# Decay steps and an expert's turning placed later, a copy placed earlier, and idle turnings on TensorE, in a streaming-encoder step

## The reference

```python
h = rms_norm(x, norm_mix); z = h @ w_in
qa, ka, va, ra, da, qb, kb, vb, ga, gb = split(z)
log_a = log_sigmoid(da @ w_decay + b_decay) / 16        # decay of the gated linear attention
o_a, s_new = gla_scan(qa, ka, va, log_a, s0)            # uses cumsum(log_a) in exponentials
...                                                     # second attention branch, gates, two projections
x = x + mix @ w_out
g = argmax over 4 groups; two best of the 4 experts in it; weights from two softmaxes
y[t] = sum over the token's 2 experts e of w * ((silu(x_t @ w_gate[e]) * (x_t @ w_up[e])) @ w_down[e])
x = rms_norm(x + y, norm_final)
```

## Time and profile before

| | before |
|---|---|
| runs (3) | median 1045.04 us, 1044.43 to 1046.35 |
| profiled execution | 1044.21 us, its span 1042.5 us |
| mean granted TensorE clock | 0.993 |
| PE busy | 1009.4 us (97%) |
| PE weight loads (PEld) | 897.5 us (86%) |
| DVE / ACT / POOL busy | 661.4 (63%) / 540.9 (52%) / 166.3 (16%) us |
| moved over the span | 207.55 MB, mean 199 GB/s |

### The profile page before, as it was taken

The page is one execution under the profiler, slowest core; times in us unless marked ns, Lnnn a source line. Parts: engine busy times, 40 slices in busy tenths (PEclk is TensorE's granted clock), DMA queues, the critical chain, the costliest instruction groups (busy, mean ns, idle before and its releaser), DMA issues.

```text
span 1042.5 us, 16960 instructions
## 1 busy us (share of the span) xinstructions
PE 1009.4 (97%) x6950; PEld 897.5 (86%) x6950; DVE 661.4 (63%) x995; ACT 540.9 (52%) x720; POOL 166.3 (16%) x178
## 2 busy tenths in 40 slices
PE   6999899999999999999999999999999999999995
PEld 5999899998999988888989899878778888888884
DVE  5334753453223356767665656356898898889896
ACT  5236533432223244545474553233677878887874
POOL 2111100000000123432331020013211011010162
PEclk9999999999999999999999999999999999999998
DMA  8877865527355465475464271616999999999976
GB/s 190 199 219 175 163 144 67 95 46 117 54 69 102 111 120 70 76 61 70 114 194 148 65 254 35 242 81 234 413 412 413 413 414 414 413 414 413 415 158 155
DMA packets 126171, 207.55 MB, mean 199 GB/s; under 512 B 11229, under 2 KB 68573, under 8 KB 126098
## 3 DMA queue, kind: packets, MB, share of 16 engines
q1 hardware_dynamic: 110290, 149.38, 53.3%
q0 software_dynamic: 13168, 47.59, 13.4%
q10 hardware_dynamic: 2640, 9.57, 2.3%
HBM read 174.40 MB, written 32.12 MB: 198 GB/s over the span
## 4 chain that ended last, share of the span: by engine, by line
PE 85%; DVE 6%; ACT 4%; issue 3%; DMA 2%; ACTq 0%; POOL 0%; DVEq 0%; POOLq 0%
PE ps L1248 23%; PE ps L1250 23%; PE ps L1249 23%; PE ps L1222 5%; PE ps L1406 2%; PE ps L1420 2%; DMA x_rows<-h,slot_i 2%; PE ps L1382 1%; ACT w_hi L848 1%; PE ps L1366 1%; PE ps L1521 1%; PE ps L1381 1%; PE ps L1318 1%; DMA xg<-x_rows 1%; DVE x L2273 0%
## 5 line engine op out<-in xcount | busy, mean ns | idle before, releaser
L1960 DVE TENSOR_TENSOR e_lo<-raw,e_hi 128x2048 fp32r<-128x2048 f32 x96 | 219.3, 2288 | 28.1 <-ACT e_hi L1031 27.9
L1031 ACT ACTIVATE e_hi<-raw 128x2048 fp32r<-128x2048 f32 x96 | 184.1, 1918 | 55.0 <-PE ps L1250 44.4
L1248 PE MATMUL ps<-h_hi,w_hi 128*128 128x272 f32 x632 | 186.7, 295 | 0.0
L1250 PE MATMUL ps<-h_hi,w_lo 128*128 128x272 f32 x632 | 182.3, 288 | 0.0
L1249 PE MATMUL ps<-h_lo,w_hi 128*128 128x272 f32 x632 | 181.9, 288 | 0.0
L1746 DVE TENSOR_TENSOR w_lo<-ring,w_hi 128x2048 fp32r<-128x2048 f32 (+1 forms) x40 | 72.5, 1812 | 79.9 <-ACT w_hi L848 79.9
L848 ACT ACTIVATE w_hi<-ring 128x1024 fp32r<-128x1024 f32 (+1 forms) x56 | 79.6, 1422 | 82.3 <-PE ps L1250 67.3
L1248 PEld LDWEIGHTS ps<-h_hi,w_hi 128*128 128x128 f32 x632 | 119.1, 188 | 1.2 <-issue 0.7
L1249 PEld LDWEIGHTS ps<-h_lo,w_hi 128*128 128x128 f32 x632 | 119.1, 189 | 0.2
L1250 PEld LDWEIGHTS ps<-h_hi,w_lo 128*128 128x128 f32 x632 | 118.8, 188 | 0.0
L1248 PE MATMUL ps<-w_hi,h_hi 128*128 128x256 f32 x384 | 109.4, 285 | 2.6 <-DVE va L2031 2.6
(11 more groups left out here) (418 smaller groups left out, 2038.8 us busy)
## 6 DMA issues: line engine op xcount, KB each, us to landing
raw<-in_w_gate_dram SPq DMA_DIRECT2D x32, 1024.0 KB, 10.3
raw<-in_w_up_dram SPq DMA_DIRECT2D x32, 1024.0 KB, 8.8
raw<-in_w_down_dram SPq DMA_DIRECT2D x32, 1024.0 KB, 9.3
ring<-in_w_in_dram SPq DMA_DIRECT2D x24, 1024.0 KB, 10.8
x_rows<-zero POOLq DMA_DIRECT2D x16, 512.0 KB, 8.0
ring<-in_w_in_dram SPq DMA_DIRECT2D x16, 512.0 KB, 8.4
xg<-x_rows POOLq DMA_DIRECT2D x15, 512.0 KB, 6.3
y_rows<-yo ACTq DMA_DIRECT2D x14, 512.0 KB, 6.6
```

Of the source, the lines that this page charges most:

```text
L1031: act.activation(e_hi[buf][:], raw[slot][:], ACT.Copy).then_inc(s_ehi, 1)
L1248: pe.matmul(out, left[0], right[0], start=first, stop=False)
L1250: return pe.matmul(out, left[1], right[0], start=False, stop=final)
L1960: dve.tensor_tensor(e_lo[slot][:], raw[slot][:], e_hi[buf][:].bitcast(F32), ALU.subtract).then_inc(s_elo, 1)
```

## The change

Four things. Two decay hooks, 3 and 4, hang behind units two later than before. ACT copies `g_row` before its second block of squares. On PE, `idle_turns` adds transposes of the identity whose results nobody uses: 44 in the entry and 10 in the last routing step. For that the wait for the identity comes first, and those ahead of the fourth tile, which write the gain's bank, wait until `g_row` is copied. In the second expert's preparation, product 3 of expert 0 comes ahead of the turning of expert 1's rows, on ACT and DVE one split of weights does so too, `rows_index` moves behind `gated`, and `overflow_counts` into expert 1.

```diff
--- before.py
+++ after.py
@@ -395,7 +395,7 @@
         hook(units_of["ra"][-1], "gate_s")
         for f in range(GH + 2):
             if f <= GH:
-                hook(units_of["va"][2 * f], "dec", f)
+                hook(units_of["va"][(0, 2, 4, 8, 10)[f]], "dec", f)
             if f >= 2:
                 hook(units_of["va"][2 * f + 1], "dec_apply", f - 2)
         for i in range(NTILE):
@@ -871,9 +871,9 @@
                 act.activation(h_hi[:, :, t0:t0 + n], ps[:, b:b + 2].rearrange("p b (c t) -> p (b c) t", t=P)[:, :, 0:n], ACT.Copy).then_inc(s_xhigh, 1)
 
             x_squares(0)
-            x_squares(1)
             act.wait_ge(s_gmix, 17)
             act.activation(g_row[:], ps[:, 0:2].rearrange("p b n -> p (b n)"), ACT.Copy).then_inc(s_gmix, 1)
+            x_squares(1)
             x_squares(2)
             x_high(0)
             x_squares(3)
@@ -1146,9 +1146,9 @@
             part_hi(third_after(0, 0))
             silu(0, part_of(0, 1), 3)
             part_hi(third_after(0, 1))
+            part_hi(third_after(0, 2))
             x_out(1, 1)
-            for j in range(2, 4):
-                part_hi(third_after(0, j))
+            part_hi(third_after(0, 3))
             body(1, 1)
             body(2, 0)
             with act.Fori(1, NE // 2 - 1) as it:
@@ -1231,14 +1231,23 @@
                 b = (4, 6, 2, 4, 6)[i]
                 transposes(n, [(ps[:, b + c // 4, P * (c % 4):P * (c % 4) + n], x0[0:n, i, P * c:P * c + P]) for c in range(KC)], s_hx)
 
-            pe.wait_ge(s_const, 1)
+            def idle_turns(count, bank):
+
+                for _ in range(count):
+                    pe.transpose(ps[:, bank, 0:P], ident[:], ident[:])
+
+            pe.wait_ge(s_const, 2)
+            idle_turns(4, 2)
             pe.wait_ge(s_gmix, 16)
             for b in range(2):
                 last = pe.matmul(ps[:, b], ones[0:1], g_one[:, 512 * b:512 * b + 512], start=True, stop=True)
             last.then_inc(s_gmix, 1)
-            pe.wait_ge(s_const, 2)
             for i in range(NTILE - 1):
+                if i == 3:
+                    pe.wait_ge(s_gmix, 18)
+                idle_turns((12, 3, 3, 14)[i], 2 if i < 3 else 0)
                 x_turn(i)
+            idle_turns(8, 0)
             pe.wait_ge(s_hT, 3)
             pe.wait_ge(s_const, 3)
 
@@ -1324,8 +1333,12 @@
                     if i:
                         last = pe.matmul(ps[:, 7, 0:NE], ones[:], cum[:, i - 1], start=False, stop=True)
                     last.then_inc(s_rank, 1)
+                    if i == NTILE - 1:
+                        idle_turns(5, 3)
                 elif what == "x_first":
                     x_first(i)
+                    if i == NTILE - 2:
+                        idle_turns(5, 3)
                 elif what == "totals":
                     pe.wait_ge(s_slot, NTILE)
                     pe.matmul(ps[:, 7, 0:NE], ones[:], cum[:, NTILE - 1], start=True, stop=True).then_inc(s_rank, 1)
@@ -1592,8 +1605,8 @@
             pe.wait_ge(s_xlo, 2)
             GU(part_of(0, 1), 0, 1, 3)
             GU(part_of(0, 2), 0, 2, 6)
+            GU(part_of(0, 3), 0, 3, 6)
             XT(1, 1, 16)
-            GU(part_of(0, 3), 0, 3, 6)
             pe.wait_ge(s_into, 3)
             slot_sums(ps[:, 7, 0:NE], [(r_hot[0:n, k * NTILE + i], ypick[0:n, k * NTILE + i]) for k in range(2) for i, (t0, n) in enumerate(TILES)])
 
@@ -2220,6 +2233,8 @@
                 part_lo(third_after(r, 1, odd))
                 if not last:
                     x_out(r + 1, 1 - odd)
+                if isinstance(r, int) and r == 1:
+                    overflow_counts()
                 part_lo(third_after(r, 2, odd))
                 if isinstance(r, int) and r in (1, 2):
                     last_one_hots(r - 1)
@@ -2237,13 +2252,12 @@
             slot_weights()
             part_lo(third_after(0, 0))
             part_lo(third_after(0, 1))
-            rows_index()
-            overflow_counts()
+            part_lo(third_after(0, 2))
             x_out(1, 1)
             gated(0, 0, 6)
             slot_weights_out()
-            for j in range(2, 4):
-                part_lo(third_after(0, j))
+            rows_index()
+            part_lo(third_after(0, 3))
             body(1, 1)
             body(2, 0)
             with dve.Fori(1, NE // 2 - 1) as it:
```

## The result

| | before | with the change |
|---|---|---|
| median, 20 executions each | 1046.55 us (1043.23 to 1050.39) | 1041.09 us (1039.18 to 1047.18) |
| ratio, 95% interval | | 0.9947 (0.9935 to 0.9959) |
| profiled execution, its span | 1044.21, 1042.5 us | 1044.18, 1042.4 us |

A forecast was written before the change was run, and what follows sets the result against it. PE, busy 97% of the 1042.5 us span, was taken as the bound, so time could come only from its waits and slow stretches. Gains 1.4 + 0.5 + 1.7 = 3.6 from 1045.04 gave 1041.4 us, range 1039.2 to 1043.9.

The forecast's parts named there:

- the sum: Entry, decay hooks and expert 1 together: 1.4 + 0.5 + 1.7 = 3.6 us gained, taken from 1045.04 us.
- the profiled execution: Basis of the sum: 1044.21 us before; the three-run median, 0.83 above it, was then used as the starting time.
- Entry, 1.4: Up to the first projection: earlier `g_row` and 44 idle turnings that raise PE's clock sooner gain 1.4 us.
- Do idle turnings count?: Whether transposes raise PE's clock: the trace's doubled rate after turnings alone says yes, the quoted skill rule no.
- the idle turnings do nothing: Rival, chance 0.11: turnings leave the clock unchanged; entry 0.5, decay 0.5, expert 1 0.4 us gained, 1043.6 us.
- Decay hooks, 0.5: Decay stage: the 2.6 us `va` wait goes, a later `ra` copy takes most back, 0.5 us is left.
- the rest is a new wait of about 2 us: Before the fourth `ra` unit: PE waits about 2 us for DVE's first `ra` sample copy.
- the decay wait goes without a new one: Rival, chance 0.13: DVE reaches the `ra` copy 2 us earlier than added up; 5.7 us gained, 1039.3 us.
- Last routing step and expert 1, 1.7: Expert 1 begins 2.8 us earlier with clock held, 1.5 with it lost; 0.95 given back for `hh`, about 1.7 left.
- the order is the old one: Behind expert 1's changes: order as before, DVE beginning expert 2 in the same step with PE as before.
- They fit with 0.1 to spare, so I cost them at nothing: Last routing step: ten idle turnings fill about 1.1 us of PE standing still, cost nothing; 0.5 late at low level.
- The rival on the other side: Slower, chance 0.06: third decay waits for a weight tile taking 16.7 us to land instead of 10.7; 1047.4 us.

The follow-up runs named there:

- the table of the 69: Executions of the unchanged kernel run beside the experiments, grouped by mean granted clock: median 1049.64 us at 0.986 to 0.987, 1043.63 at 0.994 and over.
- the spread order: Whole change with decay hook 3 one unit later instead of two, third apply at the eleventh `va` unit, fourth at the first `ra` unit: 1038.28 us, ratio 0.9924.
- the turnings in the `ra` wait: Whole change plus 22 more idle turnings on PE ahead of the fourth `ra` unit: 1043.32 us, ratio 0.9974.
- the late overflow count: Whole change with `overflow_counts` moved from expert 1 to the end of the last expert: 1040.34 us, ratio 0.9939; with decay work spread too, 1038.55 us.

## Why the prediction was right, and where not

- **Time and gain.** 1041.4 was forecast and 1041.09 measured, inside the range. The gain was 3.6 by the sum and 5.5 measured (4.3 to 6.8), and the median that it was taken from was 1.5 too low (1045.04 against 1046.55), so that the time came out to 0.3 is luck. The first step that failed is the setting of the sum against "the profiled execution" and the three runs: these had few falls of the clock. The median execution before has a mean clock of 0.991 against the profile's 0.993, and by the table of the 69 each 0.001 goes with about 0.75 us. The second is that the sum counts no falls on either side. The median clock of the change is 0.994, and 0.003 goes with some 2.2 us, about what the sum lacks. The kernel without turnings has 0.994 too, so the higher clock goes with the new order and not with the turnings; which part of the order keeps falls away is not shown.
- **Entry, 1.4.** `g_row` at 6.77 and the change of rate came as said, the latter inside the first turns in some profiles and ahead of them in others. Measured 1.07 in the profile, 1.6 in that of the entry alone (18.73 - 17.12), and 1.9 (0.4 to 3.5) in time.
- **Do idle turnings count?** For the clock they do, as the trace of before said: in the table above 1.00 from 724 to 738 us stands for five of the eight kernels with turnings there and for none of the six without. The rule that I quoted from the Trainium skill, page "TensorE: Matmul & The Clock Gate", section "Part 4: PE-mode transpose", does not agree with these turnings either: in two of the eight profiles with idle turnings in the entry the first eight real ones took 1.10 us, and before, without them, 1.96. For the time they don't, as far as these intervals tell: two pairs with and without differ by 0.02 and 0.05 us, each known to some 2 us. So the rival "the idle turnings do nothing" was wrong in its mechanism, and nearly right in that a kernel without them is as fast; its 1043.6 was not, since I had given it the whole loss of the clock.
- **Decay hooks, 0.5.** The wait for `va` went and one for `ra` came, at the place and for the reason named: "the rest is a new wait of about 2 us". It was 2.6, 1.9, 1.7 and twice 1.5 us in the profiles with this order, against the 2.0 worked out. Under-sized: in its own profile the part brings the fourth `ra` unit 1.2 us forward and not 0.6, because ACT's high half starts at 116.42 and not at 117.3, where I had put the tile's landing. The 1.9 measured for this part alone (0.3 to 3.5) allows both. What the sum missed is that the terms do not add: with PE 1.07 us ahead and the tile where it was, ACT waits 1.20 for it, and the fourth `ra` unit is only 1.15 earlier by both parts, where 1.9 had been given. The price of a fall of the clock behind such a stall is not in the term either. A fall came in two of four profiles with the `va` wait and in two of five with the `ra` wait unfilled, and put the next stage 1.3 to 1.5 us late each time. The shares are alike, so that the change makes these falls rarer is not shown. The rival "the decay wait goes without a new one" is what the spread order made true: 1038.28, where 1039.3 had been given.
- **Last routing step and expert 1, 1.7.** Shown nearly to the tenth in the profiles that it was sized for: expert 1 2.8 us earlier with the clock held (2.82), 1.5 with it lost (1.56), and 0.95 given back for `hh` (0.82). Elsewhere it depends on more than the clock: with it held but `xg` 1.46 us late (the turnings in the `ra` wait) expert 1 came 1.4 earlier, and without turnings, at 0.88, 2.9. What failed is the sentence that behind this "the order is the old one", as far as it leaves the time there as it was: the clock fell in the change's profile behind `xg`'s turning and the slot sums, and took 1.7 back. That is no price of the new order alone. Three of the four kernels with the old order fall there too, and eight of the ten with the new one (table above); the one profile that I had read, that of before, does not. "They fit with 0.1 to spare, so I cost them at nothing" held, but what they save ends in waits for `xg` and for product 3's weights (0.96, where I gave 1.4).
- **The rival on the other side**, the late tile, came in small only: the tile took 10.0 us to land, not 16.7, but was 1.20 late for ACT. That the `ra` copy's time hangs on that tile is shown by the waits above: 1.4 to 1.5 us, and what ACT waits for the tile on top.

## What to carry to other kernels

A stall that goes is worth its length only if nothing else is late next; here placing the same decay steps so that no bank copy came later than PE needed it gave 2.4 to 2.8 us more than the change had. Faster work ahead of a transfer that lands when it lands turns into waiting: with the routing turnings alone the wait for `xg` grew from 1.29 to 4.16 us. And a profile is one draw: compare stretches between profiles, and the totals between many executions, before a difference of 0.3% is explained.

The fastest kernels found are the change with the decay work spread, at 1038.3 to 1038.6 us with or without the late overflow count and the idle turnings: 0.992 to 0.9924 of the kernel before, 2.5 to 2.8 us under the change.

## What I had not expected of the hardware

The clock falls in part of the executions behind the same stall: with the same 2.6 us wait for `va` it read 1.00 from 112 to 126 us in two profiles and 0.88 in two others. The clock column read 1.00 in the entry while eight turns took 1.97 us there. And the slot sums, 2.6 us in which PE counts as busy throughout, were followed by a low stretch in 10 of 14 profiles, and ahead of the turning of `xg` where they had been moved there.
